# Dot rows turned by TensorE, the norm's factor inside gelu, and a fourth resident query head in a one-core encoder kernel

## The reference, cut to what matters

```python
def peer(xn, wq, subkeys, u, v):
    ...
        q = jnp.einsum('nd,dk->nk', xb, wq).reshape(P_TOK_BLOCK, P_HEADS, 2, P_DKEY // 2)
        s = jnp.einsum('nhcd,hckd->nhck', q, subkeys).astype(jnp.float32)
        sv, si = lax.top_k(s, P_TOPK)
        ...
        fv, fi = lax.top_k(cand, P_TOPK)
        eidx = jnp.take_along_axis(cidx, fi, axis=-1)
        g = jax.nn.softmax(fv, axis=-1)
        ue = u[eidx]
        ve = v[eidx]
        act = jax.nn.gelu(jnp.einsum('nd,nhkd->nhk', xb, ue).astype(jnp.float32), approximate=False)
        return jnp.einsum('nhk,nhkd->nd', (g * act).astype(ve.dtype), ve)
    ...
h = x + concat(A, B) @ w_o
y = h + peer(rmsnorm(h, norm2), ...)
```

## Time and profile before

| what | value |
|---|---|
| three runs | 1263.31, 1270.19, 1272.36 us (median 1270.19) |
| the profiled execution | 1266.45 us |
| its span, first to last instruction | 1264.7 us |
| PE busy | 1060.4 us (84%) |
| DVE busy | 794.4 us (63%) |
| POOL busy | 734.4 us (58%) |
| ACT busy | 356.7 us (28%) |
| DMA | 468.13 MB, mean 370 GB/s |
| mean granted TensorE clock | 0.973 |

### The profile page before, as it was taken

The page is one execution under the profiler, slowest core; times in us unless marked ns, Lnnn a source line. Parts: engine busy times, 40 slices in busy tenths (PEclk is TensorE's granted clock), DMA queues, the critical chain, the costliest instruction groups (busy, mean ns, idle before and its releaser), DMA issues.

```text
span 1264.7 us, 11354 instructions
## 1 busy us (share of the span) xinstructions
PE 1060.4 (84%) x3313; PEld 518.5 (41%) x3313; DVE 794.4 (63%) x1941; ACT 356.7 (28%) x851; POOL 734.4 (58%) x774
## 2 busy tenths in 40 slices
PE   8999989997959988777989799878868777678885
PEld 4766555654326433333543354323223222223231
DVE  1649876989567588877627466666463556563334
ACT  2535215333133342232322333121221221222110
POOL 0005545666656666667656666666666666766654
PEclk9999989998989999989999999999998999999999
DMA  9958989999999999999999999999999999999997
GB/s 379 376 202 278 413 343 367 318 378 409 405 403 408 401 366 391 373 363 366 360 409 409 409 408 383 360 358 410 409 367 348 380 354 371 371 352 371 373 372 293
DMA packets 125629, 468.13 MB, mean 370 GB/s; under 512 B 14072, under 2 KB 17152, under 8 KB 123392
## 3 DMA queue, kind: packets, MB, share of 16 engines
q0 software_dynamic: 110592, 402.70, 83.2%
q1 hardware_dynamic: 14976, 64.70, 13.1%
HBM read 462.86 MB, written 4.42 MB: 369 GB/s over the span
## 4 chain that ended last, share of the span: by engine, by line
PE 43%; DMA 21%; POOL 13%; issue 9%; DVE 8%; another core or an unknown queue 4%; ACT 1%; POOLq 0%; DVEq 0%; SPq 0%; ACTq 0%
PE PSUM L1964 21%; DMA UV<-in_p_v,EIDX 15%; POOL UV L579 7%; PE PSUM L1544 6%; POOL UV L564 6%; DMA UV<-in_p_u,EIDX 5%; PE PSUM L1553 4%; PE PSUM L1743 3%; DVE UV L1461 3%; PE PSUM L1717 2%; PE PSUM L1558 1%; PE PSUM L1565 1%; PE PSUM L1760 1%; DVE SEL L213 1%
## 5 line engine op out<-in xcount | busy, mean ns | idle before, releaser
L1964 PE MATMUL PSUM<-UV,DIAG 128*128 128x512 f32 x1500 | 728.5, 618 | 152.8 <-DMA UV<-in_p_v,EIDX 119.6
L1461 DVE CUSTOM_DVE_ANT_0 UV<-UV,PSUM 128x1024 f32<-128x1024 f32 x384 | 463.6, 1218 | 313.6 <-DMA UV<-in_p_u,EIDX 259.6
L579 POOL DMA_INDIRECT UV<-in_p_v,EIDX x376 | 360.9, 960 | 278.3 <-PE PSUM L1964 140.8
L564 POOL DMA_INDIRECT UV<-in_p_u,EIDX x384 | 364.7, 950 | 237.1 <-issue 108.2
L1964 PEld LDWEIGHTS PSUM<-UV,DIAG 128*128 128x128 f32 x1500 | 267.3, 192 | 552.4 <-issue 274.1
L996 ACT ACTIVATE DIAG<-CST,WGT 128x128 f32<-128x128 f32 x375 | 143.5, 398 | 755.4 <-PE PSUM L1964 408.8
L1544 PE MATMUL PSUM<-WR,XW 128*128 128x512 f32 (+1 forms) x128 | 50.6, 555 | 0.1
L1553 PE MATMUL PSUM<-XW,WR 128*128 128x256 f32 x192 | 46.1, 398 | 3.7 <-issue 3.7
L1553 PEld LDWEIGHTS PSUM<-XW,WR 128*128 128x128 f32 x192 | 38.4, 201 | 12.4 <-issue 6.7
L1544 PEld LDWEIGHTS PSUM<-WR,XW 128*128 128x128 f32 x128 | 24.2, 190 | 25.3 <-issue 22.7
L1461 DVE DVE_READ_ACCUMULATOR2_ANT DOTS<- 128x1 f32 x384 | 31.6, 82 | 0.0
(11 more groups left out here) (286 smaller groups left out, 831.9 us busy)
## 6 DMA issues: line engine op xcount, KB each, us to landing
WR<-in_w_o SPq DMA_DIRECT2D x13, 512.0 KB
UV<-in_p_u,EIDX POOLq DMA_INDIRECT x384
UV<-in_p_v,EIDX POOLq DMA_INDIRECT x384
WR<-in_p_wq SPq DMA_DIRECT2D x10, 512.0 KB
UV<-in_w_o SPq DMA_DIRECT2D x2, 2048.0 KB, 12.1
UV<-in_p_wq SPq DMA_DIRECT2D x2, 2048.0 KB, 9.2
WR<-in_w_B SPq DMA_DIRECT2D x2, 2048.0 KB
UV<-in_w_B SPq DMA_DIRECT2D x4, 512.0 KB, 6.5
```

The source lines that it names most:

```text
L564: nc.gpsimd.indirect_dma_start(UBUF[n % RU], None, a["p_u"], bass.IndirectOffsetOnAxis(EIDX[:, n:n + 1], 0)).then_inc(u_got[n % RU], 16)
L579: nc.gpsimd.indirect_dma_start(VBUF[m % RV], None, a["p_v"], bass.IndirectOffsetOnAxis(EIDX[:, n:n + 1], 0)).then_inc(v_got[m % RV], 16)
L1461: v.tensor_tensor_reduce(out=row, in0=row, in1=XNP, scale=1.0, scalar=0.0, op0=ALU.mult, op1=ALU.add, accum_out=DOTS[:, i % 2, s:s + 1]).t ...
L1964: ins = mm(bank[6 + k][:, :], DIAG[:, m % ND, :], VBUF[m % RV][:, k * 512:(k + 1) * 512], start=False, stop=m % SLOTS == SLOTS - 1 or m == ...
```

## The change

Four things are changed, and all else follows them.

1. `rows_for_dots` moves from DVE to PE: eight transposes of `XNT2` (already times the gain) into banks 4 and 5. For tile 0 they follow query head 1; for tiles 1 and 2 they are slots 128 and 256 of `trunk` and wait for `u_free`, the last dot of the tile before. The factor 1/rms is applied as `scale` of gelu. `NB` and its load are gone.
2. For head 0 of tile 0, DVE takes the first 8 experts from the 8 x 8 best sums after the first 8 keys of each side, ahead of keys 9 to 16. The choice of head 1 moves behind dot 0.
3. The order of the start: PE's idle matmuls no longer wait for the identity, and there are two fewer; the lower-bound rows of the recurrence come behind the second projection; ACT loads Silu's table ahead of the copies of `pt`; the states and transposed `x` of tiles 2 and 1 come later among the query heads. POOL asks for four `v` rows directly behind the first eight `u` rows, and the `v` buffers are turned by four places so that their memory is free by then.
4. Query head 4 gets a buffer of its own (`PQ`) and serves both tiles, so `load_small` has one entry less.

```diff
-RU, RV, ND = 8, 6, 6
+RU, RV, ND, EARLY = 8, 6, 6, 4
...
-            + [("wo", MIXED[1][6], 0), ("wo", MIXED[1][7], 1), ("qq", 0, 2), ("qq", 1, 0), ("qq", 2, 1), ("qq", 3, 2), ("qq", 4, 0)],
-         2: [("wo", c, n % 5) for n, c in enumerate(MIXED[2])] + [("qq", h, (8 + h) % 5) for h in range(5)]}
+            + [("qq", 4, 6), ("wo", MIXED[1][6], 0), ("wo", MIXED[1][7], 1), ("qq", 0, 2), ("qq", 1, 0), ("qq", 2, 1), ("qq", 3, 2)],
+         2: [("wo", c, n % 5) for n, c in enumerate(MIXED[2])] + [("qq", h, (8 + h) % 5) for h in range(4)]}
...
-            b = 8 - 2 * name[1] + name[2]
+            b = 6 + name[2]
...
-        return 6 * h - 12 if h < 2 else 16 * h - 18
+        return 12 * h - 12 if h < 2 else 16 * h - 18
...
-            sp.dma_start(NB[:, :], a["norm2"].partition_broadcast(P).rearrange("p o d -> p (o d)")).then_inc(n2_in, 16)
...
+            for n in range(RU):
+                if n >= 4:
+                    take(pool, ("qq", 0, n - 4))
+                gather_u(n)
+
+            for n in range(EARLY):
+                if n >= 2:
+                    take(pool, ("qq", 0, n + 2))
+                gather_v(n)
+            asked = RU
+            for n in range(EARLY, HEADS * PK):
                 while asked < min(HEADS * PK, slot_at(max(0, n - RV)) + min(n, RV) + 1):
-                    if asked == 4:
-                        take(pool, ("qq", 0, 3))
                     gather_u(asked)
                     asked += 1
-                if n == 0:
-                    take(pool, ("qq", 0, 7))
+                if n < RV:
+                    take(pool, ("qq", 0, n + 2))
                 gather_v(n)
...
             squares(0, X[0], JUNK)
+            out_bp0(0)
+            out_bp1(0)
             act.wait_ge(lb_shift, 1)
             own.done(nc.scalar.activation(SMALLC[:, 16:24], SMALLC[:, 16:24], ACT.Exp), lb_exp)
-            out_bp0(0)
-            out_bp1(0)
...
+            own.done(nc.scalar.activation(SMALLC[:, 73:74], STD1[:, 0:1], ACT.Silu))
+            copy_out(("gp", 0), SG[0], heads4, func=ACT.Silu)
             out_pt(0, 0, 0)
             out_pt(0, 1, 0)
             square_o(0)
-            copy_out(("gp", 0), SG[0], heads4, func=ACT.Silu)
+            own.done(nc.scalar.activation(SMALLC[:, 73:74], STD1[:, 0:1], ACT.Sqrt))
             copy_out(("pv", 0), MIXB, heads4)
...
-                nc.scalar.activation(GELU[:, i % 2, lo:hi], DOTS[:, i % 2, lo:hi], ACT.Gelu).then_inc(gelu_done, 1)
+                nc.scalar.activation(GELU[:, i % 2, lo:hi], DOTS[:, i % 2, lo:hi], ACT.Gelu,
+                                     scale=SMALLC[:, 9 + i // PH:10 + i // PH]).then_inc(gelu_done, 1)
...
-            def rows_for_dots(t):
-                own.done(v.scalar_tensor_tensor(out=XNP, in0=X[t], scalar=SMALLC[:, 9 + t:10 + t], in1=NB[:, :],
-                                                op0=ALU.mult, op1=ALU.mult))
...
-                    rows_for_dots(n // SLOTS)
+                    dve.wait_ge(dot_rows, n // SLOTS + 1)
...
+            def rows_for_dots(t):
+
+                if t:
+                    pe.wait_ge(u_free, SLOTS * t)
+                else:
+                    for b in (4, 5):
+                        stored(pe, [name for name in ORDER if PLACE[name][0] == b][-1])
+                for c in range(KC):
+                    ins = nc.tensor.transpose(XNP[:, c * P:(c + 1) * P], XNT2[:, c, :], IDENT)
+                ins.then_inc(dot_rows, 1)
...
-            pe.wait_ge(id_in, 16)
 
             pe.wait_ge(att_zero, 1)
             idle(8)
+            pe.wait_ge(id_in, 16)
             pe.wait_ge(x_in[0], 16)
...
-            idle(4)
+            idle(2)
...
-            first(CHOICES[0] + 5)
+            first(CHOICES[0] + 3)
+            rows_for_dots(0)
+            first(CHOICES[0] + 11)
             last_keys(0)
             new_state(0)
             turned_x(2, X[2])
+            first(CHOICES[0] + 13)
             turned_x(1, X[1])
```

More of the change, by code:

```diff
@@ L97, in product_order @@
     first = choices(0)
-    beside = first.index(("qq", 0, 3))
-    o += first[:beside] + [("ke", 0), ("u", 0)] + [("xt", t, g) for t in (2, 1) for g in range(2)] + first[beside:]
+    some, more = first.index(("qq", 0, 6)), first.index(("qq", 0, 7))
+    o += first[:some] + [("ke", 0), ("u", 0)] + [("xt", 2, g) for g in range(2)]
+    o += first[some:more] + [("xt", 1, g) for g in range(2)] + first[more:]
     o += [unit_name(*u) for u in UNITS[:8]]
@@ L201, in score_slot, with top16 @@
     return CHOICES[t] + (2 if h == 0 else 3 + 2 * h)
-def top16(own, v, rows, slot, pace):
-    for step in range(5):
+def top16(own, v, rows, slot, pace, steps=range(5)):
+    for step in steps:
         yield slot + step // pace
@@ L402, in trunk_kernel @@
             later_landed[chunk] = (s, count[s])
-        small, small_landed, before, count = [], {}, {}, [0] * 6
+        small, small_landed, before, count = [], {}, {}, [0] * 7
         for t in (1, 2):
@@ L541, in _ @@
             store_y(0)
-            for k in range(21, 29):
+            for k in range(21, 28):
                 load_small(k)
@@ L973, in _ @@
             out_xt(2)
+            first(CHOICES[0] + 14)
             out_xt(1)
@@ L1246, in choose @@
                 if (t, h) == (0, 0):
-                    own.done(v.max(FV[:, 0:8], row))
-                    own.done(v.max_index(FI[:, 0:8].bitcast(U32), FV[:, 0:8], row))
-                    yield from decode(t, h, 0, 8, slot + 1)
                     own.done(v.match_replace(out=row, in_to_replace=FV[:, 0:8], in_values=row, imm_value=PICKED))
```

68 lines of the change are left out of this document (39 added, 29 removed).

## The result

The changed kernel took 1286.91 us in the median of four runs (1283.18 to 1291.13), the kernel before 1269.64 (four runs, 1263.31 to 1272.36): a ratio of 1.0144, with a 95% interval from 1.0088 to 1.0200. The forecast was 1266.8 with 1256 to 1279, so it was wrong, and on the slow side. Its profiled execution took 1283.52 (span 1281.7).

A forecast was written before the change was run, and what follows sets the result against it. PE was taken to bound the kernel from 116 us, DMA from about 270 us to the end. Terms summed to -1.5 us: 1266.45 gave 1264.95, plus 1.9 for run spread 1266.8, range 1256 to 1279 for 8 in 10.

The forecast's parts named there:

- The start: Prologue: PE's idle matmuls run while the identity comes, so `AF`'s matmuls and all behind start earlier; -2.5 us, ends 0 and -3.4.
- ACT's tables: Prologue: the Silu copy leaves its place ahead of the copy of `MIXB`; -0.4 us, ends 0 and -1.9.
- The dot rows of tile 0: Behind query head 1: eight transposes now on PE's path; +1.6 us, ends +0.8 and +3.2.
- The -0.9 for PE's waits: First query head to units: PE's waits for ACT's copies go with split copies; ends 0 and +1.0.
- First gathers: Start of POOL's gathers: about 5.4 us sooner, but the wait for the first expert sum grows; 0, other end -7.
- Rival (a): Up to 175 us gathers, not PE, set the pace: 7 us more gained, 1259.8 us; chance 0.10.
- The dot rows of tile 1: Slot 128: PE waits 9.0 us for dot 127, then transposes 1.6; +2.0 us, ends 0 and +10.6.
- rival (c): PE's wait at slots 128 and 256 counts in full and the queue runs dry: 11.6 us more, 1278.4; chance 0.12.
- At slot 256: Dot rows of tile 2: PE waits 1.4 us for dot 255 and transposes 1.6; 0, ends 0 and +3.0.
- Loads: One 512 KB query head load goes where DMA limits: -1.3 us; `NB`'s load goes in the prologue: 0.
- Rival (b): PE's stall from about 162 to 166.70 us, in the units, is gone: 7.4 us less, 1259.4; chance 0.13.
- Within 1%: Whole kernel: chance 0.80 of a time within 1% of before; 0.14 faster and 0.06 slower by over 1%.

The follow-up runs named there:

- s8: The changed kernel with stands (small idle copies on ACT) ahead of heads 5 and 7 and once in every 14 expert sums: 1219.81 us.
- s10: s8 with both last output projection blocks issued ahead of `kt` and PE's dot rows of tiles 1 and 2 three slots later: 1216.85 us.
- s13: s8 with both last output projection blocks of the second tile issued ahead of `kt`, nothing else: 1219.60 us.
- s14: s8 with PE's dot rows of tiles 1 and 2 at slots 131 and 259, nothing else: 1216.46 us.
- s11: s10 with last keys, state and transposed `x` back behind head 2's query (tile 1's `x` one head later than in the kernel before): 1211.42 us.
- s2: The changed kernel with the first four `v` rows asked for behind the first 29 `u` rows: 1198.49 us against 1198.83 for the kernel before.
- s1: The changed kernel with the last output projection block issued ahead of `kt` again: 1198.02 us against 1198.83 for the kernel before.
- s3: The changed kernel with PE's dot rows of tiles 1 and 2 at slots 131 and 259: 1196.53 us against 1198.83 for the kernel before.

## Why the prediction was wrong

**The start** was right: -2.7 at `AF` for the -2.5, -3.0 at the first query head for -2.9, which has the -0.4 for ACT's tables in it.

**The dot rows of tile 0, and the stretch from the first head to the units: the step that failed first.** The prediction gives this stretch +0.7 (1.6 - 0.9) and bounds it at +4.2; on the first chip it grew by 15.9. The transposes took 1.04 us, not 1.6. The -0.9 for PE's waits, with +1.0 at most "if ACT's copies of tile 1 now hold up the last head", rested on ACT being free. On chip 5 the stretch from the first head to the units is 27.3 us against 26.3 before, +0.9 where +0.7 was said, and the units start at 113.30 for the 113.9 forecast. On the first chip it is 43.3 us against 27.35: ACT stood, and the change had moved the work that the units need from behind head 2 to behind head 5, so that the copies of heads 3 to 5 and the stands ahead of them now came first. I had a trace before me in which ACT stood 3.34 us before 111.87 and PE some 4 us between 162.2 and 166.70, and I let no term stand for what a stand costs in the new order. s8, s10, s13 and s14 show that cost for a stand at head 5: 4.3 to 6.7 us at `v` row 12, and from s10 to s11 the old order takes 4.4 away. On the first chip the lag there was 5.3. That the order makes it so there is argued, not shown by a run on it: the changed kernel's ACT also stood longer ahead of its units, 16.2 us against 3.34. Whether that is chance or comes of the earlier and denser gathers (theory B) stays open; in both traces the first stand lies behind the first gather.

**First gathers: 0** was right on chip 5. There the units are 1.38 sooner and so is `v` row 12 (1.37), though the first gather comes 4.8 sooner. s2 changes nothing on chip 7. Rival (a) falls there.

**The dot rows of tile 1: +2.0, mis-sized.** PE's wait of 9.0 was measured as 9.21. What I priced by POOL's next row alone holds the sums of six `v` rows: on the first chip the lag grew by 4.5 and DMA fell to 259 GB/s, on chip 5 by 3.3 with 320 GB/s, with stands by 3.7 (s8). On chip 5 it was given back within 60 rows; with stands s14 wins 3.1 us against s13 by three slots' delay. The mechanism is rival (c)'s; its 10.6 us for this slot came out as 3.3 to 4.5. At slot 256 PE had no wait, on the first chip and on chip 5, as forecast within its bounds.

**Loads: -1.3** counted bytes and didn't follow SP's list entry by entry, and so missed that a block slid behind 1 MB. The wait is real, 11.70 us here and 10.28 on chip 5, and worth nothing that can be told from 0 by s1 and s13. On the first chip the lag grew by 7.1 us between `v` rows 48 and 60: no wait on "remote" lies between 345 and 364 us, and POOL's 14.57 us of wait before 364.28 end with the sums behind the block. DMA was still full then, 404 GB/s from 340 to 400 us. It falls only behind that, to 354 GB/s from 400 to 450, where an ACT stand of 8.48 us ends at 404.75 and a POOL stand of 3.37 at 404.90. On chip 5 DMA stayed full from 340 to 440 us. So the block put POOL behind, and bytes were lost later, where stands came on top; how much of these 6 us is the block's stays open, since no run was on a chip on which it shows.

**Rival (b)** came true on the first chip, since the units lasted 50.4 us there, and it is the rule on chip 5, where the kernel before has 50.35 (114.68 to 165.03) as well. The same two packets of instructions are on DMA from 160 to 165 us on chip 5, with no pause of PE, and on the first chip ACT stood at the same time (8.54 us until 166.94). So here the rule of the Trainium skill (Runtime: NRT & Kernel Launch, Instruction fetch mechanics: fetching is mostly hidden) agrees with the trace, and the pause of the earlier trace rows wasn't the program's. That the change's loss on the first chip is 5.3 us at the sums, and not 12.9, is owed to this pause and not to the forecast.

**The range.** Within 1%, with 0.80, is what the changed kernel does on the two other chips on which it ran as it is, and not on the one that was measured. I took the kernel's own spread (1263 to 1272) for all the spread there is, and gave 0.06 to slower although the trace showed 60 waits that no part of the program ended. What the prediction lacked is a term for a moved step that meets such a wait.

## What to carry to other kernels

Where a trace has pauses that no instruction explains, price each moved step twice, once as it is and once with an engine standing for five microseconds ahead of it: work that the next stage needs belongs ahead of work that can wait, even if both orders are equal when nothing stands. An in-order engine that waits at a fixed slot for another's last result should get two or three independent pieces of work ahead of that wait (s3 against s1, s14 against s13: 0.1 to 0.3%). And when a list of loads grows in its middle, follow each later entry past every other transfer on its queue.

## What the runs showed of the hardware

The kernel before took 1269.6 us on one chip and 1198.7 to 1199.4 on five others, with the same traffic: DMA moved 368 GB/s against 407 (chip 5) from 1000 to 1100 us. The slower trace has the 218 us of waits on "remote", chip 5's has none; several engines come out of one together. What sends them is open. The instruction packets alone don't, since both chips have 61 of them, and on chip 7 a full gather queue didn't (s1, s3). On the first chip the gathers aren't ruled out: the first stand begins behind the first gather in both traces (gathers from 99.78 and 94.31, stands from 104.8 and 97.1).

The Trainium skill (DMA: Bandwidth & Descriptors, Measured (HBM→SBUF, 128 partitions, SWDGE, issued from GpSimd)) says that a core gets about 358 GB/s when the other core of its memory domain streams too. The first chip's mean of 364 to 369 GB/s over the span lies near it, but its stretches reach from 259 (460 to 480 us of the changed kernel) to 410; no run here decides whether a neighbour was at work.

Behind its wait for a stand at head 5, PE was at the lower clock level. Eight matmuls of 128x128 behind 6.79 us of wait took 2.08 us in s8, and 1.16 behind 0.95 us in s11.
